# Attention units of a hybrid block in one run behind the first conv group, instead of spread over 24 groups

## What is computed

```python
h = rms_norm(x, norm_mix)
proj = h @ w_in            # columns: x_in, b_g, c_g (512 each) | q, k, v (512 each) | gate_a, gate_b (1024 each)
y_conv = short_conv_mixer(x_in, b_g, c_g, conv_w) @ w_out_conv      # b_g * conv3(c_g * x_in)
q = rms_norm(q per head, q_norm); k = rms_norm(k per head, k_norm)
y_attn = neighbourhood_attention(q, k, v, rpb) @ w_out_attn
mixed = sigmoid(gate_a) * y_conv + sigmoid(gate_b) * y_attn
x = x + mixed @ w_o
```

## Time and profile before

| | |
|---|---|
| median of 3 runs | 2538.66 us (2538.42 to 2540.11) |
| the profiled execution | 2538.22 us |
| its span | 2536.3 us |
| TensorE busy | 2378.2 us (94%) |
| VectorE busy | 1452.1 us (57%) |
| ScalarE busy | 1040.1 us (41%) |
| GpSimd busy | 912.9 us (36%) |
| mean granted clock of TensorE | 0.969 |

### The profile page before, as it was taken

One profiled execution on the slowest core, in us unless ns is written; L12 is line 12 of the kernel. 1 busy time (PEld: TensorE's weight loads), 2 busy tenths in 40 slices (PEclk: granted clock), 3 DMA queues, 4 the chain that ended last, 5 costly groups with the idle time before them and its releaser, 6 DMA issues.

```text
span 2536.3 us, 34875 instructions
## 1 busy us (share of the span) xinstructions
PE 2378.2 (94%) x11094; PEld 1519.6 (60%) x11095; DVE 1452.1 (57%) x1855; ACT 1040.1 (41%) x1053; POOL 912.9 (36%) x514
## 2 busy tenths in 40 slices
PE   8997999999999994599999999999999999999996
PEld 4443444456666553377766666666667666666774
DVE  3201333341111224488887777778778777778885
ACT  2111212231101001267664556556556565555664
POOL 3210111100000001466745444546546545445663
PEclk9998999999999996699999999999999999999998
DMA  4114110001111323489988788889889888788995
GB/s 150 67 41 109 33 42 25 22 20 50 49 26 58 124 88 128 154 298 352 340 315 271 261 311 277 290 286 306 289 310 313 286 300 289 269 302 289 323 340 166
DMA packets 180116, 505.32 MB, mean 199 GB/s; under 512 B 18082, under 2 KB 60578, under 8 KB 180066
## 3 DMA queue, kind: packets, MB, share of 16 engines
q1 hardware_dynamic: 163874, 457.97, 50.6%
q0 software_dynamic: 16192, 46.67, 8.3%
HBM read 468.34 MB, written 32.05 MB: 197 GB/s over the span
## 4 chain that ended last, share of the span: by engine, by line
PE 78%; DVE 9%; issue 6%; ACT 2%; DVEq 1%; POOL 1%; DMA 1%; SPq 1%; ACTq 0%; POOLq 0%; PEldq 0%
PE psum L1423 12%; PE psum L1425 11%; PE psum L1424 11%; PE psum L1235 7%; PE psum L1292 6%; PE psum L1326 4%; PE psum L1434 4%; PE psum L1370 4%; DVE w_lo L1090 3%; PE psum L1338 2%; PE psum L1337 2%; PE psum L1336 2%; PE psum L1276 2%; PE psum L1469 2%; PE psum L1264 1%
## 5 line engine op out<-in xcount | busy, mean ns | idle before, releaser
L1090 DVE TENSOR_TENSOR w_lo<-ring,w_hi 128x2048 fp32r<-128x2048 f32 x384 | 874.9, 2309 | 85.5 <-ACT w_hi L714 71.9
L714 ACT ACTIVATE w_hi<-ring 128x2048 fp32r<-128x2048 f32 x384 | 721.3, 1919 | 179.6 <-DMA ring<-in_w_down 94.2
L555 POOL TENSOR_SCALAR pick<-iota_bf,slot_col 128x256 bf16<-128x256 bf16 x272 | 514.8, 1905 | 62.5 <-DVE slot_col L1106 62.4
L1423 PE MATMUL psum<-w_hi,xT_hi 128*128 128x512 f32 x1024 | 424.4, 414 | 36.6 <-DVE w_lo L1090 31.5
L1425 PE MATMUL psum<-w_hi,xT_lo 128*128 128x512 f32 x1024 | 407.4, 398 | 0.0
L1424 PE MATMUL psum<-w_lo,xT_hi 128*128 128x512 f32 x1024 | 406.9, 397 | 0.0
L561 POOL DMA_INDIRECT xg<-h_rows,idx_new x33 | 83.8, 2539 | 585.6 <-issue 539.8
L1423 PEld LDWEIGHTS psum<-w_hi,xT_hi 128*128 128x128 f32 x1024 | 193.7, 189 | 157.4 <-issue 64.7
L1425 PEld LDWEIGHTS psum<-w_hi,xT_lo 128*128 128x128 f32 x1024 | 193.9, 189 | 47.2
L1424 PEld LDWEIGHTS psum<-w_lo,xT_hi 128*128 128x128 f32 x1024 | 194.6, 190 | 39.9
L1423 PE MATMUL psum<-w_hi,aT_hi 128*128 128x512 f32 x512 | 214.4, 419 | 3.3 <-DVE aT_lo L1130 3.3
(11 more groups left out here) (237 smaller groups left out, 3076.1 us busy)
## 6 DMA issues: line engine op xcount, KB each, us to landing
ring<-in_w_gate SPq DMA_DIRECT2D x256, 512.0 KB, 5.2
ring<-in_w_up SPq DMA_DIRECT2D x256, 512.0 KB, 6.4
ring<-in_w_down SPq DMA_DIRECT2D x256, 512.0 KB, 5.7
ring<-in_w_in SPq DMA_DIRECT2D x28, 512.0 KB, 4.7
ring<-in_x SPq DMA_DIRECT2D x16, 512.0 KB, 4.0
ring<-in_w_in SPq DMA_DIRECT2D x6, 1024.0 KB, 7.4
vb<-oT SPq DMA_DIRECT2D x16, 256.0 KB, 6.5
ring<-in_w_o SPq DMA_DIRECT2D x4, 1024.0 KB, 6.0
```

The costliest lines, as they stand in the source:

```text
L555: e.tensor_scalar(pick[:, t, :], iota_bf[:, :], slot_col[:, t, :], None, ALU.is_equal).then_inc(g_pick, 1)
L714: e.activation(w_hi[:, hs, :], ring[:, slot, :], ACT.Copy).then_inc(g_hi, 1)
L1090: e.tensor_tensor(w_lo[:, hs, :], ring[:, slot, :], w_hi[:, hs, :].bitcast(F32), ALU.subtract).then_inc(g_lo, 1)
L1423: e.matmul(dst, hi, w_up, start=start, stop=False)
```

## The change

All units are put behind group 0 (`unit_end`). The transposes and products of a unit come one unit later in TensorE's order (un - 2 and un - 3), and so do the copies of the transposes on ScalarE and of the results on VectorE. `prob` has three buffers instead of two; `probT`, `nmin`, `rsum`, `rinv` and the PSUM banks stay at two. `min_of(n)` now waits for the transpose of unit n - 3 instead of n - 2. The 23 groups that follow have no units between them, and the drain has one unit more.

```diff
--- before.py
+++ after.py
@@ -187,8 +187,8 @@
         junk = ypre[:, 3, :]
         sq = rb_[:, 0:512]
         qn = [rb_[:, 512:1024], rb_[:, 1024:1536]]
-        prob = [rb_[:, 0:384], rb_[:, 384:768]]
-        probT = [rb_[:, 768:1152], rb_[:, 1152:1536]]
+        prob = [rb_[:, 384 * i:384 * i + 384] for i in range(3)]
+        probT = [rb_[:, 1152 + 384 * i:1152 + 384 * i + 384] for i in range(2)]
         u = [ra[:, 0:1024], ra[:, 1024:2048]]
         tmp = [ra[:, 512 * i:512 * i + 512] for i in range(4)]
         xe = [rb_[:, 0:1024], rb_[:, 1024:2048]]
@@ -330,7 +330,7 @@
         NCONST = 7
 
         units = HEADS * 8
-        unit_end = [(m + 1) * units // 24 for m in range(24)]
+        unit_end = [units for m in range(24)]
 
         def unit(n):
             h, b = n // 8, n % 8
@@ -648,7 +648,7 @@
 
             def exps(n):
                 e.wait_ge(smin, n + 1)
-                e.activation(prob[n % 2], prob[n % 2], ACT.Exp, bias=nmin[:, n % 2:n % 2 + 1], scale=-1.0,
+                e.activation(prob[n % 3], prob[n % 3], ACT.Exp, bias=nmin[:, n % 2:n % 2 + 1], scale=-1.0,
                              accum_out=rsum[:, n % 2:n % 2 + 1]).then_inc(sexp, 1)
 
             def probs_out(n):
@@ -666,9 +666,10 @@
                     e.activation(u[j % 2][:, 512 * hf:512 * hf + 512], bank[m % 2][:, :], ACT.Copy).then_inc(uev, 1)
                 while un < unit_end[m]:
                     exps(un)
-                    if un:
-                        probs_out(un - 1)
+                    if un >= 2:
+                        probs_out(un - 2)
                     un += 1
+            probs_out(units - 2)
             probs_out(units - 1)
 
 
@@ -865,18 +866,18 @@
                 h, rb, cb, v = unit(n)
                 e.wait_ge(sc, n + 1)
                 e.wait_ge(bias_ok, 6 * h + v + 1)
-                if n >= 2:
-                    e.wait_ge(ptr, n - 1)
+                if n >= 3:
+                    e.wait_ge(ptr, n - 2)
                 if n == 0:
                     e.wait_ge(qtr, 2 * TT)
-                e.tensor_tensor_reduce(out=prob[n % 2], in0=bank[2 + n % 2][:, 0:KEYS], in1=bias[:, v, :], scale=1.0,
+                e.tensor_tensor_reduce(out=prob[n % 3], in0=bank[2 + n % 2][:, 0:KEYS], in1=bias[:, v, :], scale=1.0,
                                        scalar=3.0e38, op0=ALU.add, op1=ALU.min, accum_out=nmin[:, n % 2:n % 2 + 1]).then_inc(smin, 1)
 
             def normalise(n):
                 e.wait_ge(sexp, n + 1)
                 e.reciprocal(rinv[:, n % 2:n % 2 + 1], rsum[:, n % 2:n % 2 + 1]).then_inc(sinv, 1)
                 e.wait_ge(sinv, n + 1)
-                e.tensor_scalar(prob[n % 2], prob[n % 2], rinv[:, n % 2:n % 2 + 1], None, ALU.mult).then_inc(snorm, 1)
+                e.tensor_scalar(prob[n % 3], prob[n % 3], rinv[:, n % 2:n % 2 + 1], None, ALU.mult).then_inc(snorm, 1)
 
             def attn_out(n):
                 h, rb, cb, v = unit(n)
@@ -911,10 +912,11 @@
                     e.tensor_tensor(ypre[:, j, cols], bank[m % 2][:, :], ypre[:, j, cols], ALU.mult).then_inc(bmul, 1)
                 while un < unit_end[m]:
                     min_of(un)
-                    if un >= 2:
-                        attn_out(un - 2)
+                    if un >= 3:
+                        attn_out(un - 3)
                     normalise(un)
                     un += 1
+            attn_out(units - 3)
             attn_out(units - 2)
             attn_out(units - 1)
 
@@ -1261,7 +1263,7 @@
                 if n >= 2:
                     e.wait_ge(pev, n - 1)
                 for i in range(3):
-                    ins = e.transpose(bank[4 + n % 2][:, P * i:P * i + P], prob[n % 2][:, P * i:P * i + P], ident[:, :])
+                    ins = e.transpose(bank[4 + n % 2][:, P * i:P * i + P], prob[n % 3][:, P * i:P * i + P], ident[:, :])
                 ins.then_inc(ptr, 1)
 
             def weighted(n):
@@ -1296,11 +1298,13 @@
                     e.sem_inc(w_used, 1)
                 while un < unit_end[m]:
                     scores(un)
-                    if un >= 1:
-                        prob_transpose(un - 1)
                     if un >= 2:
-                        weighted(un - 2)
+                        prob_transpose(un - 2)
+                    if un >= 3:
+                        weighted(un - 3)
                     un += 1
+            prob_transpose(units - 2)
+            weighted(units - 3)
             prob_transpose(units - 1)
             weighted(units - 2)
             weighted(units - 1)
```

## The result

The changed kernel takes 2617.41 us (median of 5 runs, 2615.52 to 2617.61) against 2540.11 (5 runs) for the kernel before beside it: a ratio of 1.0304, 95% interval 1.029 to 1.0318. It is slower by 77 us, and 3.9 us above the forecast. The profiled execution took 2617.58 us, span 2615.6.

A forecast was written before the change was run, and what follows sets the result against it. TensorE's order of work was taken to bound the middle stage. Start, low-clock run, conv groups and drain moved the merge from 545.28 to 620.6 us, +75.3 on 2538.22, so 2613.5 us, range 2590 to 2624.

The forecast's parts named there:

- The start: Before the run: group 0 begins at 190.32 us, and unit 0's product waits for vb until 221.73, as now.
- The run: The unit stretch on TensorE: 60 gapless steps of 3.865 us at the low clock, ending at 455.1 us.
- Third buffer and distance: Probability tile wait on L879, 17.9 us at most, goes; counted as nothing, 0.26 us a unit only at the high clock.
- Rival D: In the run: the change of distance does nothing at the low clock; part of the forecast, moves no time, no separate chance.
- Conv groups, drain and merge: Behind the run: 23 groups 158.0 us, freed weights 2.4, first group's low clock 1.2, drain 3.4 and 0.5; merge at 620.6.
- The sum: Whole kernel: the merge starts at 620.6 against 545.28 us, so +75.3 us, giving 2613.5 us.
- Rival A: In the run: the high clock comes back early, steps of 2.12 us, 2508.6 us in total; chance 0.10.
- B: In the run: the high clock comes back late, results from 2515 to 2600 us, of either sign; chance 0.07.
- C: In the run: VectorE and ScalarE or the bias become the bound, 2620 us and above; chance 0.03.
- that the run is entered at the low clock: At unit 0's product: the clock is low after some 19 us in which TensorE has had little to do.

The follow-up runs named there:

- experiment 1: The changed kernel with 16 more conv passes, result unused, between the wait for vb and the product of unit 0: 2519.38 us, ratio 0.9922.
- experiment 4: The kernel before, old distance and two probability buffers, with only the order changed, all units behind group 0: 2621.29 us, ratio 1.032.
- experiment 8: The kernel before, old distance and two buffers, with units 0 to 2 behind group 2 and all others behind group 4: 2511.67 us, ratio 0.9892.
- experiment 5: The changed kernel with the old order, units spread over the groups, so distance and third buffer alone: 2525.17 us, ratio 0.9945.
- experiment 6: As experiment 5, with ScalarE copying the transposes of un - 2 before the exponential of un: 2506.98 us, ratio 0.9874.
- experiment 2: The changed kernel with all units behind group 4 instead of group 0: 2601.87 us, ratio 1.0246.
- experiment 10: The changed kernel with 128 columns of V instead of 64 as the products' stationary side: 2605.6 us (one run).
- experiment 9: The changed kernel with scores over all 128 rows of qkT instead of 64, adding a head pair's scores: 2505.34 us (one run).

## Why the prediction was right

*The start.* As forecast: nothing of vb's path moved, the fill was over early, and the product of unit 0 waited until 222.95 (forecast 221.73). Of the 1.2 us, 0.8 were there before the stage: the first conv group began at 191.1 and not 190.3.

*The run.* 60 steps of 3.880 us against 3.865 forecast, 0.9 us in all. The two gapless steps of rows 5 (3.85 and 3.88) were a fair sample of sixty. This one term, 105 us of low clock, set the sign, and experiment 1 shows it by adding nothing but a burst that brings the clock back: 98 us less.

*Third buffer and distance.* Counted as nothing at the low clock, and experiment 4 has the same step of 3.880 us without them. Rival D was right for the changed kernel. Where the clock is high I had put 0.26 us a unit on it, read from stretches of three units between conv groups; in a long run that holds for half of the heads, and the mean is 0.20 (experiment 8). The 17.9 us of rows 2 were mostly the long waits behind the convolution, and those need ScalarE's order changed too (experiments 5 and 6).

*Conv groups, drain and merge.* From the last product's end (457.19) to the merge (623.71) 166.5 us against 165.5 forecast. The waits for freed weights were 2.1 us over 7 groups and 0.3 at the last; none waited for weights. Two errors were of opposite sign: the first group was at the low clock for 0.9 us, which costs about 0.5 and not the 1.2 that I took, and a group behind a group took 6.93 us and not 6.87 (four groups in the 28.01 us from 493.10 to 521.11, less one wait of 0.30), 1.3 us over 23 groups.

*The sum.* The merge began at 623.7, forecast 620.6: 1.2 from the start, 0.9 from the steps, 1.0 from the groups. What is left up to 3.9 is behind it.

*Rival A* was the Trainium skill's rule (sustained activity releases the throttle, "TensorE: Matmul & The Clock Gate", Part 1 and its closing table). By that rule the run would have taken about 127 us instead of 233; the run was busy for 234.1 of 234.1 us at 0.50, so the rule does not hold for this stream. It had 0.10. It fails over sixty units in four different kernels (the changed one and experiments 2, 4 and 10). *B* and *C* did not come about; the bias never held a unit up.

One step was right for a wrong reason: that the run is entered at the low clock. I took it from the stall of some 19 us for vb. A stall can do it (in experiment 6, behind gapless work, the clock fell 1.4 us into the wait), but in the changed kernel the clock fell at 202.2, in the fill, before the wait began, and in experiment 2 it fell with no wait for vb at all. In experiment 1, up to the wait the same instructions as the changed kernel, it fell at 203.7, one microsecond into the wait. That vb was late is therefore not what the low clock hangs on.

## What to carry to other kernels

Before work is gathered into one run, look at the clock that its own instruction mix gets, by entering it both ways: here the same 60 steps take 127 us or 233. Fill a pipeline between dense groups, so that the run starts with every piece ready, and put the copy that the matrix engine waits for ahead of the instruction that waits for a slow producer. Here the order of ScalarE's queue was worth 18 us, and the third buffer with the distance 14 without it.

## What was not expected of the hardware

- Gapless matrix work stayed at 1.2 GHz for all of its 234.1 us in the changed kernel. Of the shapes tried, the scores with 64 rows held it there; with 128 rows, and the other pieces as they were, the clock was at 1.00 some 3 us into the run. The transposes and the products with 64 columns did not hold it down then. With the high clock given, the 64-row scores kept it (127 us in experiment 1).
- The clock can fall without a long stall. Right behind a conv group it fell after the scores of four units, the transposes of two and 1.8 us of gaps (experiment 2), and in the changed kernel after a stretch in which TensorE was busy for 3.4 of 3.9 us (198.2 to 202.1).
- How soon conv passes brought it back differed: after 0.9 us behind the run of the changed kernel, after 3.9 behind the same run of experiment 4, and after 5.8 in the burst of experiment 1 (221.7 to 227.5).
- 64 stationary columns are dearer than 128 here: with V on 128 columns, like the transposes beside it, a step takes 0.20 us less at 1.2 GHz and 0.11 to 0.13 less at 2.4 GHz. Scores over 128 rows made it 0.15 us less at 2.4 GHz (experiment 9). Whether the cause is the change of shape from piece to piece, or the shape itself, was not tried.
